# Twelve of the 32 expert places of a sparse layer narrowed to 64 tokens, and three stages joined in one block

## The reference, cut to what matters

```python
def moe_ffn(xn, router_w, router_b, w_gate_up, b_gate_up, w_down, b_down):
    logits = (xt @ router_w).astype(jnp.float32) + router_b
    top_v, top_i = lax.top_k(logits, TOP_K)          # TOP_K 4 of 32
    top_w = jax.nn.softmax(top_v, axis=-1)
    ...
    h = lax.ragged_dot(xs, w_gate_up, group_sizes) + b_gate_up[e_sorted]
    gate, up = h[:, :D_FF], h[:, D_FF:]              # D_FF 1024
    gate = jnp.minimum(gate, SWIGLU_LIMIT)
    up = jnp.clip(up, -SWIGLU_LIMIT, SWIGLU_LIMIT)
    a = (up + 1.0) * (gate * jax.nn.sigmoid(SWIGLU_ALPHA * gate))
    y = lax.ragged_dot(a, w_down, group_sizes) + b_down[e_sorted]
```

## Time and profile before

| what | value |
|---|---|
| median of 3 runs | 2262.12 us (2259.86 to 2262.86) |
| the profiled execution | 2262.05 us |
| its span | 2259.8 us |
| PE busy, share of the span | 97% |
| DVE, ACT busy | 70%, 58% |
| DMA traffic in the span | 515.71 MB |
| weights of the experts | 384 loads of 1024 KB |

### The profile page before, as it was taken

One profiled execution on the slowest core, in us unless ns is written; L12 is line 12 of the kernel. 1 busy time (PEld: TensorE's weight loads), 2 busy tenths in 40 slices (PEclk: granted clock), 3 DMA queues, 4 the chain that ended last, 5 costly groups with the idle time before them and its releaser, 6 DMA issues.

```text
span 2259.8 us, 30266 instructions
## 1 busy us (share of the span) xinstructions
PE 2196.7 (97%) x10198; PEld 1782.0 (79%) x10198; DVE 1578.8 (70%) x1697; ACT 1303.7 (58%) x1528; POOL 301.3 (13%) x398
## 2 busy tenths in 40 slices
PE   6999899999999999998899999999999999999998
PEld 6888677876667888887578888888888888888886
DVE  6777444754344334346598888989888898988886
ACT  5666443442224433233387777777777777777774
POOL 3334100202320000001011011110101101011110
PEclk9999999999999999998699999999999999999999
DMA  4110332321113333344599999999999999999993
GB/s 185 57 56 28 118 106 89 116 65 38 47 38 112 118 114 131 95 147 184 212 347 368 375 364 364 371 361 367 369 370 359 363 372 362 366 373 366 364 365 128
DMA packets 89010, 515.71 MB, mean 228 GB/s; under 512 B 15108, under 2 KB 16132, under 8 KB 38184
## 3 DMA queue, kind: packets, MB, share of 16 engines
q1 hardware_dynamic: 79448, 498.05, 59.4%
q0 software_dynamic: 9216, 16.81, 3.1%
q10 hardware_dynamic: 288, 0.09, 0.0%
HBM read 508.59 MB, written 23.33 MB: 235 GB/s over the span
## 4 chain that ended last, share of the span: by engine, by line
PE 67%; DVE 1%; issue 0%; DMA 0%; ACT 0%; POOL 0%; POOLq 0%; DVEq 0%; ACTq 0%
PE bank L2185 15%; PE bank L2187 15%; PE bank L2186 15%; PE bank L1717 5%; PE bank L1719 5%; PE bank L1718 5%; PE bank L2206 1%; PE bank L2196 1%; PE bank L2237 1%; PE bank L1754 1%; PE bank L1756 1%; PE bank L1755 1%; PE bank L2221 0%; DVE moe_lo L2176 0%; PE bank L1781 0%
## 5 line engine op out<-in xcount | busy, mean ns | idle before, releaser
L2176 DVE TENSOR_TENSOR moe_lo<-moe_raw,moe_hi 128x2048 fp32r<-128x2048 f32 x382 | 855.1, 2285 | 11.6 <-ACT moe_hi L2169 10.6
L2169 ACT ACTIVATE moe_hi<-moe_raw 128x2048 fp32r<-128x2048 f32 x380 | 728.6, 1919 | 166.3 <-PE bank L2187 160.4
L2185 PE MATMUL bank<-moe_hi,moe_XTh 128*128 128x512 f32 x1024 | 404.5, 395 | 0.0
L2186 PE MATMUL bank<-moe_lo,moe_XTh 128*128 128x512 f32 x1024 | 404.3, 395 | 0.0
L2187 PE MATMUL bank<-moe_hi,moe_XTl 128*128 128x512 f32 x1024 | 404.2, 395 | 0.0
L168 ACT ACTIVATE unit_hi<-unit_raw 128x1024 fp32r<-128x1024 f32 x116 | 122.2, 1059 | 237.7 <-DMA unit_raw<-in_w_units 231.6
L174 DVE TENSOR_TENSOR unit_lo<-unit_raw,unit_hi 128x1024 fp32r<-128x1024 f32 x116 | 145.8, 1262 | 159.6 <-ACT unit_hi L168 159.1
L2187 PEld LDWEIGHTS bank<-moe_hi,moe_XTl 128*128 128x128 f32 x1024 | 193.5, 189 | 44.6
L2186 PEld LDWEIGHTS bank<-moe_lo,moe_XTh 128*128 128x128 f32 x1024 | 193.5, 189 | 44.5
L2185 PEld LDWEIGHTS bank<-moe_hi,moe_XTh 128*128 128x128 f32 x1024 | 194.2, 190 | 40.4
L2185 PE MATMUL bank<-moe_hi,moe_aTh 128*128 128x512 f32 x512 | 199.5, 390 | 0.5 <-DVE moe_lo L2176 0.5
(11 more groups left out here) (365 smaller groups left out, 3642.0 us busy)
## 6 DMA issues: line engine op xcount, KB each, us to landing
moe_raw<-in_w_moe SPq DMA_DIRECT2D x384, 1024.0 KB, 6.9
unit_raw<-in_w_units SPq DMA_DIRECT2D x116, 512.0 KB, 3.5
da_slab<-in_w_qkv SPq DMA_DIRECT2D x8, 1536.0 KB, 6.8
y_caT<-in_x SPq DMA_DIRECT2D x4, 512.0 KB, 5.6
yda_d<-y_daT SPq DMA_DIRECT2D x1, 2048.0 KB, 6.3
y_daT<-in_blocks_qk SPq DMA_DIRECT2D x1, 2048.0 KB, 11.1
y_daT<-yda_d SPq DMA_DIRECT2D x1, 2048.0 KB, 8.1
y_daT<-in_x SPq DMA_DIRECT2D x1, 2048.0 KB, 8.7
```

What stands on the lines that cost most here:

```text
L2169: nc.scalar.activation(HI[ring(n, pos)][:], RAW[pos][:], ACT.Copy).then_inc(s_hi, 1)
L2176: nc.vector.tensor_tensor(LO[pos][:], RAW[pos][:], HI[ring(n, pos)][:].bitcast(F32), ALU.subtract).then_inc(s_lo, 1)
L2185: nc.tensor.matmul(bank[:], xh[:, x], HI[ring][:, w], start=start and k == 0, stop=False)
L2186: nc.tensor.matmul(bank[:], xh[:, x], LO[pos][:, w], start=False, stop=False)
```

## The change

A place of the expert loop is now a position in an order, not an expert's number. The router's counts are ranked on the chip: DVE compares each expert's count, times 64 plus a tie number, with all others, a product with the expert numbers writes the order into `K.order`, and every engine that needs an expert's number (SP, POOL) loads it from there (`expert`). Expert 0 is always first. The 20 places of highest count stay as they were. The 12 of lowest count are small: 64 tokens. For these a tile holds the rounded part of the 64 tokens in columns 0 to 63 and their rest in columns 64 to 127, so that `unit` makes two products per slice and not three (one with w_hi, one with w_lo, both with the same stationary tile). Rows 0 to 63 of the bank then hold the rounded part's result and rows 64 to 127 the rest's; ACT copies the bank to `fold` (`to_fold`), and PE adds both halves by a plain float32 product with `onto`, two identities under each other (`fold_down`). An expert has six banks, hence six folds. An expert of a small place with more than 64 tokens would go to the overflow path.

The turn is written out for ten places per loop body (`SMALL`), three times round. `down` of one expert lies in the next one's turn, as before.

The stages `ca`, `ml` and `mix` now share one block, with explicit waits where the barrier stood. `mlcols` is loaded at the start of the kernel.

```diff
+NS = 64
+SMALL = (0, 1, 0, 1, 0, 0, 1, 0, 1, 0)
...
-            sp.dma_start(mlcols[:], A["mlcols"]).then_inc(s_hc, 16)
+        sp.wait_ge(K.s_ca_y, 4 * CAH // 2)
             sp.dma_start(wif, A["w_if"]).then_inc(s_wif, 16)
...
             for g in range(AHEAD):
+            act.wait_ge(K.s_ca_x, g + 1)
                 keep_x(g)
...
+        pool.wait_ge(K.s_ca_y, 4 * CAH // 2)
             nc.gpsimd.memset(xm[:, :, 0:3], 0.0).then_inc(s_pad, 1)
...
+        pe.wait_ge(K.s_ml_pjk, K.n_ml_pj)
             for i in range(2):
                 step(i, i, 0, 2 * i, YDA, KT, YDA if i == 0 else None)
...
+        for t in range(TT):
+            mm = nc.tensor.matmul(K.banks[2][0:NE, NE:2 * NE], K.ones[:, 0:NE], ind[:, t, :], start=(t == 0),
                                       stop=(t == TT - 1))
...
+        nc.vector.scalar_tensor_tensor(keys[:], K.banks[2][0:NE, NE:2 * NE], 64.0, tie, ALU.mult, ALU.add)
             chain(nc.vector.tensor_copy(cnt[:], K.banks[2][0:NE, 0:1]))
+        chain(nc.vector.scalar_tensor_tensor(key[:], cnt[:], 64.0, tiec, ALU.mult, ALU.add))
+        chain(nc.vector.tensor_scalar(above[:], keys[:], key[:], None, ALU.is_gt))
+        chain(nc.vector.tensor_reduce(rank[:], above[:], AX, ALU.add))
+        nc.vector.tensor_scalar(seated[:], seat, rank[:], None, ALU.is_equal).then_inc(s_seat, 1)
+        chain(nc.vector.tensor_scalar(less[:], rank[:], NBIG - 0.5, float(P - NS), ALU.is_gt, ALU.mult))
+        nc.vector.tensor_scalar(K.orec[:].rearrange("p (b f) -> p b f", f=2)[:, :, 1], orow, less[:], None, ALU.subtract)
+        chain(nc.vector.tensor_tensor(cnt[:], cnt[:], less[:], ALU.add))
...
+    def expert(eng, n):
+
+        return eng.value_load(K.order[0:1, ds(n, 1)], min_val=0, max_val=NE - 1)
...
+        if small:
+            for k in range(4):
+                w = slice(k * HF, (k + 1) * HF)
+                x = slice((k0 + k) * P, (k0 + k + 1) * P)
+                nc.tensor.matmul(bank[:], xh[:, x], HI[ring][:, w], start=start and k == 0, stop=False)
+                mm = nc.tensor.matmul(bank[:], xh[:, x], LO[pos][:, w], start=False, stop=stop and k == 3)
+            mm.then_inc(s_use, 1)
+            return
...
+    def fold_down(pe, f, bank):
+
+        pe.wait_ge(s_fc, 1)
+        pe.wait_ge(s_fk, f + 1)
+        nc.tensor.matmul(bank[0:NS, :], onto[:], fold[:], start=True, stop=True).then_inc(s_fd, 1)
+
+    def to_fold(act, f, bank, ready):
+
+        act.wait_ge(s_use, ready)
+        act.wait_ge(s_fd, f + 1)
+        nc.scalar.activation(fold[:], bank[:], ACT.Copy).then_inc(s_fk, 1)
...
+                op = nc.vector.tensor_tensor(high(x), low(Yb[i][:]), low(x).bitcast(F32), ALU.subtract)
...
+                ups(0, 0)
+                if prev:
+                    fold_down(pe, g + 3, Hb[3])
+                ups(0, 1)
+                if not prev:
                 turn_a(pe, n - 1, 1)
+                ups(1, 0)
+                if prev:
+                    turn_a(pe, n - 1, 1)
+                if cur:
+                    fold_down(pe, f, Hb[0])
+                ups(1, 1)
...
+                downs(4)
+                if cur:
+                    fold_down(pe, f + 1, Hb[1])
+                pe.wait_ge(s_aTl, START + n * 2)
+                downs(5)
+                downs(6)
+                if prev:
+                    fold_down(pe, g + 4, Yb[0])
+                downs(7)
                 turn_a(pe, n, 0)
+                ups(2, 0)
+                if prev:
+                    fold_down(pe, g + 5, Yb[1])
+                ups(2, 1)
                 if more:
                     turn_x(pe, n + 1)
+                ups(3, 0)
+                if cur:
+                    fold_down(pe, f + 2, Hb[2])
+                ups(3, 1)
```

More of the change, by code:

```diff
@@ new lines, in stage_ca, with _ @@
+    block = K.block
+    K.s_ca_x, K.s_ca_y, K.s_ca_yk = s_xu, s_y, s_yk
+    @block.sync
+    def _(sp):
+        sp.dma_start(K.yda_d, K.y_daT[:]).then_inc(s_yd, 16)
+        for u in range(8, 28):
+            group, i = (u - 4) // 4, u % 4
+            if i < 3:
+                sp.wait_ge(s_use, 3 * (group - 1) + i + 1)
+            else:
+                sp.wait_ge(s_row, NR * (group // 3) + (0, 4, 6)[group % 3])
+            refill(K, sp, u // 4, i)
+        for g in range(AHEAD):
+            sp.wait_ge(s_xu, g + 1)
+            refill(K, sp, 7, g)
+        sp.wait_ge(s_yd, 16)
@@ L2177, in lo, with unit @@
                                 ALU.subtract).then_inc(s_lo, 1)
-    def unit(pe, done, pos, ring, bank, xh, xl, k0, start, stop):
+    def unit(pe, done, pos, ring, bank, xh, xl, k0, start, stop, small=0):
         pe.wait_ge(s_lo, done)
+        if small:
[4 more added lines that the diff above has]
+                mm = nc.tensor.matmul(bank[:], xh[:, x], LO[pos][:, w], start=False, stop=stop and k == 3)
+            mm.then_inc(s_use, 1)
+            return
         for k in range(4):
@@ L2345, in overflow, with turns @@
                 body(i, NE + i)
+    def turns(it, turn):
+        at = lambda k: it * sum(SMALL) + sum(SMALL[:k])
+        for k in range(len(SMALL)):
+            turn(it * len(SMALL) + (k + 1), (k + 1) % 2, True, SMALL[k], SMALL[k - 1], SMALL[(k + 1) % len(SMALL)],
+                 at(k) * 6, at(k - 1) * 6 if k else None)
     with nc.Block(no_gpsimd_drain=True) as block:
@@ L2350, in refill @@
             def refill(n, first=False):
+                here, ahead = None if first else expert(sp, n), expert(sp, n + 1)
                 for pos in range(12):
@@ L2397, in _ @@
             up(pe, 0, 0, 3, places(0, 10))
-            with pe.Fori(0, NE // 2 - 1) as pair:
-                turn(pair * 2 + 1, 1, True)
-                turn(pair * 2 + 2, 0, True)
+            with pe.Fori(0, 3) as it:
+                turns(it, turn)
             turn(NE - 1, 1, False)
@@ L2448, in turn @@
+                    if slot == 11 and cur:
+                        silu(act, n, 1, f + 4, 1)
                     ahead(n, slot)
@@ L2463, in _ @@
                 hi(act, 1, pos)
-            with act.Fori(0, NE // 2 - 1) as pair:
-                turn(pair * 2 + 1, 1, True)
-                turn(pair * 2 + 2, 0, True)
+            with act.Fori(0, 3) as it:
+                turns(it, turn)
             turn(NE - 1, 1, False)
@@ L2586, in _ @@
                 lo(dve, 1, pos)
-            with dve.Fori(0, NE // 2 - 1) as pair:
-                turn(pair * 2 + 1, 1, True)
-                turn(pair * 2 + 2, 0, True)
+            with dve.Fori(0, 3) as it:
+                turns(it, turn)
             turn(NE - 1, 1, False)
@@ L2684, in program @@
             stage_mix(K)
+            shared.close()
             K.forget_sems()
@@ L2765, in layouts @@
     out["ove"] = np.tile(np.array([[0, NE * CAP]], np.int32), (OVER, 1))
+    seats = np.empty(NE, np.float32)
+    seats[[i for i in range(NE) if not KINDS_OF[i]] + [i for i in range(NE) if KINDS_OF[i]]] = np.arange(NE)
+    ties = NE - 1 - np.arange(NE) + (1 << 20) * (np.arange(NE) == 0)
+    sort = np.zeros((NE, 2 * NE + 5), np.float32)
+    sort[:, 0:NE], sort[:, NE:2 * NE], sort[:, 64], sort[:, 65] = ties, seats, ties, np.arange(NE)
+    sort[:, 66:69] = np.arange(NE)[:, None] * CAP + P * np.arange(1, 4)
+    out["sort"] = sort
     out["lim"] = np.tile(np.array([[P, 2 * P, 3 * P]], np.float32), (NE, 1))
```

2336 lines of the change are left out of this document (1198 added, 1138 removed).

## The result

The changed kernel takes 2233.65 us (median of 4 runs, 2231.48 to 2234.45); the kernel before took 2261.84 us beside it (2259.86 to 2262.86). The ratio is 0.987, 95% interval 0.9858 to 0.9883. The change is faster by 28 us; 67 were predicted, and the time lies above the range.

A forecast was written before the change was run, and what follows sets the result against it. PE was taken to bound the kernel. From 2262.05 us, less 64 for the experts (68 less 4 for waits), 2.2 and 2.0 for the seams, plus 1.3 for the ranking, came 2195.2, stated as 2195 us; range 2183 to 2220.

The forecast's parts named there:

- What bounds the kernel: Expert loop: PE sets the pace, 35.75 us a turn, with DVE, ACT and the loads close behind.
- the first rival: Expert turns: DVE or ACT becomes the bound, keeping DVE's waits; 2241 us, or 2217 at half; region 2208 to 2245, chance 0.15.
- What the change removes: PE, small experts: four products fewer in each of 8 up and 4 down units, 11.1 us per expert.
- the split between the two turns: Small expert's pair of turns: the `cur` turn falls to about 31.0 us, the next to about 34.8.
- What it adds: PE, small experts: six plain float32 folds at 0.90 us each (0.86 to 1.0), 5.4 us per expert.
- the 4 us set aside for waits: Twelve small experts: PE's waits for ACT's fold copies, 4 us in all (0 to 25).
- the longer loop body: Expert loop's jumps: costed at nothing, since PE shows no gap at the present loop's jumps.
- Whether DVE and ACT follow: Pair of turns: DVE needs about 62 us against PE's 65.8, ACT has slack; the copies' cover holds narrowly.
- The loads: Expert weights: 390 GB/s needed at a mean turn of 33.6 us, 420 GB/s taken as possible; costed at nothing.
- The clock: Rival, around folds: PE's granted clock falls; one dip in each of 24 turns gives 2352 us; chance 0.04.
- The seams: PE gaps between `ca`, `ml` and `mix`: -2.2 us at the first, -2.0 at the second.
- The ranking: Router, before the experts: more PE products and DVE operations, +1.3 us (0.7 to 3); loads from `K.order` covered.

The follow-up runs named there:

- run 4: The changed kernel with each fold's float32 product issued twice, writing the same result again: 2297.16 us, ratio 1.0149.
- run 1: The changed kernel with all thirty turns written out, without a loop on PE, ACT, POOL or DVE: 2212.82 us, ratio 0.978.
- run 2: The changed kernel with no small place and no fold, still ten turns per loop body: 2278.83 us, ratio 1.0069.
- run 3: The changed kernel with no small place and no fold, two turns per body, fifteen times round: 2257.24 us, ratio 0.9976; repeated, 2254.65 us.
- run 5: The changed kernel with the same number of small places in a body of five turns, six times round: 2265.02 us, ratio 1.0013.
- run 11: The changed kernel with no small place, four turns per body, seven times round, two turns written out: 2256.03 us, ratio 0.997.
- run 6: The changed kernel with fifteen small places, two turns per body, the last pair written out: 2203.98 us, ratio 0.9745.
- run 8: The changed kernel with fifteen small places, two turns per body, and the fold as a float32r product: 2163.12 us, ratio 0.9559.
- run 12: The changed kernel with twelve small places, all turns written out, and the fold as a float32r product: 2172.44 us, ratio 0.9597.

## Why the prediction was off, by its own steps

**What bounds the kernel: right.** PE sets the pace before and after. It has no idle time between the returns. The time, 2233.65, lies where the first rival put its region (2208 to 2245), but by chance: that rival wanted PE to wait for DVE or ACT.

**What the change removes, 11.1 us per small expert: right.** 3.8 us are left of it with six folds of 1.21 us: 3.8 + 7.3 = 11.1. As a by-product, the split between the two turns was wrong. `turn_x` stands ahead of bank 3's unit, so the distance that ends in a small expert's turn holds six of its up units and two folds, 5.6 - 2.4 = 3.2 us less (35.75 to 32.6, measured 32.65), and the next one its last two, the down units and four folds, 5.5 - 4.8 = 0.7 less (35.02 to 35.26 measured). The prediction gave 31.0 and 34.8; the sum of the pair doesn't depend on it.

**What it adds, the first failed step: "a fold costs 1.0 us at most. I take 0.90".** A fold costs 1.21 us. The floor, 0.86, was the marginal price in a row of the same form, and run 4 confirms it for a second fold behind a first. The mistake was the bound above it: one change of kind, 0.09 us, on each side of that floor. Measured are 0.10 and 0.11 on the sides and 1.00 inside a pair that stands alone, 0.14 above the floor. What these 0.14 consist of no run shows; a short wait of the weight load on "issue" stands at nearly every fold (24.4 us in 68 cases, at most 0.4). 6 x 0.31 x 12 = 22 us of the missing gain; the 4 us set aside for waits, which didn't come, gave part of it back.

**The second failed step: "the longer loop body I cost at nothing too, since PE shows no gap at the present loop's jumps".** The trace of before did show a loop without a gap, but a loop of two turns, and the conclusion to ten has no row behind it; the prediction should have bounded it. Measured: 18.6 us for two returns in the traces, 20.8 between the medians of run 1 and the changed kernel. Of the first one's 9.6 us, 7.9 are the stop and 1.6 the products at the 1.2 GHz level behind it: six at 0.43 instead of 0.23 us and a slow bias product. Runs 1, 2, 3, 5 and 11 tie it to returns of bodies of five turns and more. Why a long body stops PE and a short one doesn't, no run shows directly.

The Trainium skill (Runtime: NRT & Kernel Launch, Instruction fetch mechanics) says that each engine holds few instructions, 2048 on PE, reads on ahead in sequence, and must fetch by DMA before it goes on when a branch goes to an instruction that it doesn't hold. The trace agrees in kind: the stop is on PE's own issue, and the instruction queue reads 75 to 84 packets in kernels that return from a long body against 35 to 41 with bodies of two or four turns. The written-out kernels read 69 and 68 without a stop, so it isn't the amount that is read: what the stop goes with is the return. The Trainium skill gives no price, for which the runs have 7.2 to 8.7 us of stop.
**Whether DVE and ACT follow: right, and better than allowed for.** The 4 us for waits on ACT's copies weren't needed; PE has no idle time before a fold. The first rival falls: DVE, busy for 271 of 300 us between the returns, never stopped PE.

**The loads: right for this kernel, with less room than the prediction had.** 383 to 387 GB/s flow with no wait for a load (the changed kernel and run 6). The Trainium skill (DMA: Bandwidth & Descriptors, Where 436 GB/s comes from) sees the limit at about 358. These rates lie above it, and the measurement decides. But "at 420 GB/s" was read from slices of 3 us; over 900 us runs 8 and 12 reach 402 and 399 with ACT waiting for loads. Had the folds cost 0.90 and the returns nothing, the mean turn of 33.6 us would have needed 390, close under it.

**The clock: right.** It is 1.00 in the turns between the returns. From 1180 us on a dip appears only at the stops.

**The seams: right in sum, -4 predicted.** In the profiled execution of after, the stages ahead of the first seam ended 1.9 us later (last product of `ca` at 389.67 against 387.77; the clock was 0.91 against 0.96 in the first 40 us, with the same work; why is open). Against that start `ml` gains 3.45 us (its last transposes begin at 686.13 instead of 687.68): 2.2 for the gap, and the rest for seven products at half clock that stood behind it, which the prediction hadn't counted. `mix` gives 1.35 more instead of 2.0: the router's first count is 2.9 us earlier in all, at 1067.13 instead of 1070.03. The branch product starts at 696.72 where it stood at 701.30, and not at the 699.7 of the prediction, since seven gate products ran at half clock behind the old gap of 4.58 us. But the new wait for the split, 2.58 us, has eight products at half clock behind it, 1.6 us, and these gave part of it back.

**The ranking: 1.3 predicted, about 0.5 measured in the trace.** Router 2.9 us earlier, experts 2.4 us earlier. PE's new counting took 0.6 us and not 2.0, and fell wholly in time in which DVE was preparing (L1849 ends at 1071.3, the lists wait for DVE until 1071.90). The gather lands near 1082.0, 4.5 us after its issue, and PE, ACT and DVE start together at 1082.8: the start now hangs on the meeting of the engines behind DVE's last operation at 1081.06, and not on the gather. A load from `order` takes 0.27 us on SP and 0.29 us on POOL, inside the bounds and covered. 384 loads: no overflow.

**The sum again**, with the two terms as measured: 45.1 us saved by twelve experts, 18.6 lost at two returns, 1.1 saved in the first two turns, which the sum didn't have, and 2.4 before them: 30.0.

## What to carry to other kernels

A lone product of another kind costs more than its distance in a row of its kind: add both changes and what the row hides (here 0.90 became 1.21), or make it of the same kind (0.23). A short loop without a gap says nothing of a long one: ask what the body holds in instructions, and what one return would cost against the gain of each pass; here the same twelve narrow places in a written-out loop, or fifteen in a body of two turns, keep what the returns took. A resource with no waits in the present profile needs its limit measured where it binds, over a long stretch, before the next gain is promised.

## What the runs showed of the hardware that was not expected

- A return of a loop with a body of five or ten turns stops PE for 7.2 to 8.7 us (thirteen returns in five kernels) and leaves it at half clock for about 3 us; bodies of two and four turns don't stop it, and neither do thirty turns written out.
- A gap of 2.19 us on PE at the old seam was followed by seven products at 0.43 us instead of 0.23, so removing it gave 3.45 us. The same stood behind a wait of 2.58 us at the start of `mix`: eight products at 0.43 us.
- Here the DMA engines' busy share doesn't tell the room left: 0.99 at 366 and at 383 GB/s, 1.01 at 402. The time to landing does: 6.9 us in the earlier trace rows, 7.8 after, 18.3 where the loads bind.
- POOL's indirect DMA of the finished rows takes 3.5 us in the changed kernel (median of 32) where it took 1.6; it is off the path, and no run was made to find out why.
